# Prompt attention of a hybrid trunk layer: ScalarE scales the mixed values at the head of the next step, VectorE inverts the sums one step sooner

## The reference, cut to what matters

```python
def fox_block(qb, cq, q_pos, k, v, ck, k_pos):
    s = jnp.einsum('bqhd,bshd->bhqs', qb.astype(jnp.float32), k) * DH_F ** -0.5
    s = s + jnp.swapaxes(cq, 1, 2)[..., :, None] - jnp.swapaxes(ck, 1, 2)[..., None, :]
    s = jnp.where(k_pos[None, :] <= q_pos[:, None], s, -jnp.inf)
    p = jax.nn.softmax(s, axis=-1)
    return jnp.einsum('bhqs,bshd->bqhd', p, v).astype(qb.dtype)
```

## Time and profile before

| what | value |
|---|---|
| median of 3 runs | 4860.73 us (4858.03 to 4862.85) |
| the profiled execution | 4847.97 us, of it 4846.3 us from the first to the last instruction |
| granted TensorE clock, mean of the program | 0.929 |
| first attention stage, steps | about 420 to 535 us |
| second attention stage, steps | about 1837 to 2548 us |

### The profile page before, as it was taken

One profiled execution on the slowest core, in us unless ns is written; L12 is line 12 of the kernel. 1 busy time (PEld: TensorE's weight loads), 2 busy tenths in 40 slices (PEclk: granted clock), 3 DMA queues, 4 the chain that ended last, 5 costly groups with the idle time before them and its releaser, 6 DMA issues. The chain is left out here.

```text
span 4846.3 us, 48883 instructions
## 1 busy us (share of the span) xinstructions
PE 4326.4 (89%) x16974; PEld 2666.9 (55%) x16974; DVE 3032.4 (63%) x6385; ACT 969.1 (20%) x1863; POOL 1260.3 (26%) x969
## 2 busy tenths in 40 slices
PE   8996686989999987888887988869999999999988
PEld 5554453665555545666663766654545455444534
DVE  1002351458777767989881487766889777877743
ACT  1112221111101104555541122220000000000023
POOL 0000031014444442333320000004444444444410
PEclk9998788999999997878878999989999999999999
DMA  4443496769999988978858777749999999999941
GB/s 166 144 146 103 143 320 280 279 245 422 379 386 391 374 337 279 343 286 308 331 218 322 291 256 258 239 149 417 419 404 410 419 419 419 415 415 412 412 184 58
DMA packets 363495, 1477.73 MB, mean 305 GB/s; under 512 B 38338, under 2 KB 178418, under 8 KB 242706
## 3 DMA queue, kind: packets, MB, share of 16 engines
q0 software_dynamic: 119872, 824.76, 42.4%
q1 hardware_dynamic: 193874, 625.13, 34.8%
q10 hardware_dynamic: 49536, 25.17, 1.7%
HBM read 1369.00 MB, written 115.38 MB: 306 GB/s over the span
## 5 line engine op out<-in xcount | busy, mean ns | idle before, releaser
L2552 POOL DMA_INDIRECT ex_uv<-in_uv,idx x768 | 1169.7, 1523 | 1706.2 <-DVE ex_acc L2609 1512.5
L2593 DVE CUSTOM_DVE_ANT_0 ex_uv<-ex_uv,ex_xp 128x1024 f32<-128x1024 f32 x768 | 912.8, 1222 | 290.6 <-DMA ex_uv<-in_uv,idx 243.4
L2609 DVE SCALAR_TENSOR_TENSOR ex_acc<-ex_uv,ex_wt,ex_acc 128x1024 f32<-128x1024 f32 x768 | 943.5, 1282 | 10.8 <-DVE C L893 3.2
L392 PE MATMUL proj_psum_acc<-proj_w,aT_later 128*128 128x385 f32 x2304 | 748.8, 487 | 7.7 <-DMA proj_w<-in_w_in 7.7
L2807 PE MATMUL exp_psum_dn<-exp_dn_big,exp_dn_gg 128*128 128x512 f32 x1536 | 685.1, 596 | 28.7 <-DVE exp_dn_gg L2763 28.6
L2798 PE MATMUL exp_psum_dn<-exp_dn_xT,exp_dn_big 128*128 128x384 f32 x2048 | 683.2, 487 | 6.9 <-DMA exp_dn_big<-in_ud 6.9
L392 PEld LDWEIGHTS proj_psum_acc<-proj_w,aT_later 128*128 128x128 f32 x2304 | 437.0, 190 | 319.1 <-DMA proj_w<-in_w_in 7.9
L2798 PEld LDWEIGHTS exp_psum_dn<-exp_dn_xT,exp_dn_big 128*128 128x128 f32 x2048 | 390.0, 190 | 306.4 <-issue 69.5
L2807 PEld LDWEIGHTS exp_psum_dn<-exp_dn_big,exp_dn_gg 128*128 128x128 f32 x1536 | 291.0, 191 | 379.1 <-issue 351.8
L301 PE MATMUL proj_psum_acc<-proj_w,aT 128*128 128x385 f32 x1152 | 377.4, 488 | 4.5 <-DMA proj_w<-in_w_in 2.6
L301 PEld LDWEIGHTS proj_psum_acc<-proj_w,aT 128*128 128x128 f32 x1152 | 218.5, 190 | 159.4 <-issue 5.1
(11 more groups left out here) (460 smaller groups left out, 4241.7 us busy)
## 6 DMA issues: line engine op xcount, KB each, us to landing
proj_w<-in_w_in SPq DMA_DIRECT2D x48, 1540.0 KB, 10.4
rt_w<-in_w_q SPq DMA_DIRECT2D x36, 2048.0 KB, 8.4
exp_dn_big<-in_ud SPq DMA_DIRECT2D x128, 512.0 KB
exp_dn_big<-in_vd SPq DMA_DIRECT2D x128, 512.0 KB
scratch_z<-proj_zs SPq DMA_DIRECT2D x216, 192.5 KB, 2.0
rt_w<-in_w_br_m SPq DMA_DIRECT2D x18, 2048.0 KB, 9.0
rt_w<-in_w_br_f SPq DMA_DIRECT2D x18, 2048.0 KB, 8.9
rt_w<-in_w_out SPq DMA_DIRECT2D x18, 2048.0 KB, 8.0
```

What stands on the lines that cost most here:

```text
L392: mm = pe.matmul(acc[j % SLOTS][:, 0:CW], aT[:, k, t * P:(t + 1) * P], w[:, u % U, k, :], start=(k == 0), stop=(k == KD - 1))
L2552: pool.indirect_dma_start(self.uv[:, slot, :], None, self.uv_tab, bass.IndirectOffsetOnAxis(ap=self.idx[:, at:at + 1], axis=0)).then_inc(s ...
L2593: dve.tensor_tensor_reduce(self.uv[:, slot, 0:D], self.uv[:, slot, 0:D], self.xp[:], 1.0, 0.0, ALU.mult, ALU.add, self.dot[:, g % 2, j:j + ...
L2609: dve.scalar_tensor_tensor(out=self.acc[:, j % 2, :], in0=self.uv[:, slot, D:2 * D], scalar=self.wt[:, g % 2, j:j + 1], in1=self.acc[:, j ...
```

## The change

The scaling leaves VectorE: `act_y` does it on ScalarE with a Copy whose scale is the inverted sum, at the head of turn s+2, ahead of the heads, the mLSTM slot and the copies. The reciprocal stays on VectorE and moves from turn s+2 to turn s+1, behind the maximum of s+1 (`dve_invert`). It now waits for `y_ready` of two steps before, whose buffer of the inverse it writes over. ScalarE's loop has one turn more and VectorE's one less. TensorE, GpSimd and SyncE are as they were.

```diff
-    def dve_y(self, dve, s):
+    def dve_invert(self, dve, s):
+        dve.wait_ge(self.expd, s + 1)
+        if s >= 2:
+            dve.wait_ge(self.y_ready, s - 1)
+        dve.reciprocal(self.inv[:, s % 2:s % 2 + 1], self.total[:, s % 2:s % 2 + 1]).then_inc(self.inverted, 1)
+
+    def act_y(self, act, s):
         hd, b = divmod(s, self.NB)
         i, e = divmod(hd, 2)
-        dve.wait_ge(self.expd, s + 1)
-        dve.reciprocal(self.inv[:, s % 2:s % 2 + 1], self.total[:, s % 2:s % 2 + 1]).then_inc(self.inverted, 1)
-        dve.wait_ge(self.inverted, s + 1)
-        dve.wait_ge(self.mixed, s + 1)
+        act.wait_ge(self.inverted, s + 1)
+        act.wait_ge(self.mixed, s + 1)
         if i >= 2:
-            dve.wait_ge(self.y_out[i % 2], i // 2 * 16)
-        dve.tensor_scalar(self.y[:, i % 2, b, e * DF:(e + 1) * DF], self.y_ps[:, 0:DF], self.inv[:, s % 2:s % 2 + 1],
-                          None, ALU.mult).then_inc(self.y_ready, 1)
+            act.wait_ge(self.y_out[i % 2], i // 2 * 16)
+        act.activation(self.y[:, i % 2, b, e * DF:(e + 1) * DF], self.y_ps[:, 0:DF], ACT.Copy,
+                       scale=self.inv[:, s % 2:s % 2 + 1]).then_inc(self.y_ready, 1)
...
         def _(act):
...
-            for s in range(STEPS + 1):
+            for s in range(STEPS + 2):
+                if s >= 2:
+                    fx.act_y(act, s - 2)
                 if s < STEPS:
                     for hd, g in fx.heads_at(s):
                         fx.act_head(act, hd, g)
                     ml.act_slot(act, *slot(s, 0))
-                if s >= 1:
+                if 1 <= s <= STEPS:
...
         def _(dve):
...
-            for s in range(STEPS + 2):
+            for s in range(STEPS + 1):
                 if s < STEPS:
                     fx.dve_max(dve, s)
-                if s >= 2:
-                    fx.dve_y(dve, s - 2)
+                if s >= 1:
+                    fx.dve_invert(dve, s - 1)
```

## The result

The changed kernel takes 4826.11 us (median of 3 runs, 4822.48 to 4826.2), against 4860.73 before. The ratio is 0.9924, with a 95% interval of 0.9909 to 0.9939.

A forecast was written before the change was run, and what follows sets the result against it. In the second attention stage no single engine bounds, waits between engines decide. 15.3 - 2 + 2 - 2 + 1 = 14.3 us gain: 4833.7 against the profiled execution, 4846.4 us against the median; range 4829 to 4863.

The forecast's parts named there:

- VectorE's side: Second attention stage: without the scaling, VectorE saves 0.30 us in 51 of 95 intervals, 15.3 us, less 2 for new waits.
- TensorE's side: Second attention stage: the 46.7 us wait for `y` all but vanishes, but little reaches the next scores; +2 us.
- act_exp` no longer waits for the reciprocal behind its maximum: Exponentials on ScalarE: dropping their wait for the reciprocal gains under 0.1 us in a dozen steps; +1 us.
- ScalarE's side: Second attention stage: 96 new Copies of 0.31 us, mostly covered by ScalarE's waits for transposes; -2 us.
- The first stage: First attention stage: VectorE half idle, only 2.0 us of waits for `y`; 0 us, between -2 and +2.
- The base: Whole kernel: forecast from one profiled execution, 4847.97 us, with the median shown 12.8 us above it.
- The low end of the range: Whole kernel: 4829 us, given as the middle of the second rival and as what VectorE's upper bound gives.
- the second rival: TensorE, second attention stage: waits for `y` end, granted clock rises above 0.80; gain about 30 us, 4831; chance 0.12.
- VectorE's upper bound: Second attention stage: VectorE's saving of 0.30 us counts in all 96 steps, 28.8 us.
- the signs listed: Profile signs, mainly second stage: VectorE about 28 us less busy, hardly any `y` wait, stage 14 us shorter, clock within 0.03.

## Why the prediction was wrong

**VectorE's side: right, as far as it can be priced alone.** 0.30 us a step was forecast. In the 38 intervals from maximum to maximum that VectorE carries in both timelines, 12.8 us are gone, 0.33 each. The rule of the Trainium skill ("VectorE: DVE Perf Modes", "The DRAIN you can't avoid"), by which a step would save 0.20 us, doesn't hold for these tiny instructions. (The section also says that a next operation which is not held starts earlier; the start 0.07 us behind the reciprocal agrees with that.) Putting the slot back costs 19 us where 15.3 was the term. But the slot's price too depends on the other chains: with the table load held, the kernel that scales on ScalarE is only 6 us ahead of the one that scales on VectorE ahead of the maximum (4842.9 and 4848.4), and with the load free it is 12 (4823.6 and 4835.7). The two differences themselves lie within each other's noise.

**TensorE's side: the step that failed.** "What it wins is the part that reached the next scores", put at +2. The reading of the earlier trace rows was that an earlier mix "would not have brought the next scores forward at all", because they hang on the exponentials. That was true of the timeline as it stood, where mix and exponentials end 0.2 us apart, but the change moves both: by 0.61 and 0.35 us on the mean, and the next scores by 0.44. The other half of the mistake is the term "`act_exp` no longer waits for the reciprocal behind its maximum, worth under 0.1 us in a dozen steps: +1". I priced the reciprocal's 0.15 us, and overlooked that a table load of 1.28 us stands between that wait and the exponentials, and so could never run beside the maximum. The two terms together were 3 us. The reciprocal moved alone brings 20, and `y` ahead of the maximum as well brings 24, all of it still on VectorE (some 5 of either may be VectorE's, by the estimate above); the wait put back into the changed kernel takes 19. What stays open is why the freed wait brings nothing (3 us) while `y` still stands behind the reciprocal, and 20 as soon as it is 0.2 us sooner.

**ScalarE's side: right in kind, perhaps too low.** Forecast -2 for the first Copy; a second one costs 9, at the edge of the noise. The two are not the same thing, since the second comes on top, but it hints that the cover was thin.

**The first stage** was put at 0, and no run contradicts it beyond its error.

**The base** was off as well. Granted TensorE clock and length of the stage vary with the same program: 0.80 and 695.1 us in the earlier trace rows, 0.77 and 0.78 with 709.8 and 706.6 in the other two. Going back from the profiled execution to the median was right, but the counts of waits were those of a short execution, and from their mean the stage lost 30.1 us, not 23.0. The low end of the range doesn't follow from its own reasons either: the second rival stands at 4831, and VectorE's upper bound gives 4860.7 - 28.8 = 4831.9, not 4829. The measured 4826.1 lies below all three.

**Clock.** The second rival (y-waits end, the clock rises, 4831) comes nearest to the outcome; it had 0.12. Of the 30.1 us, TensorE's busy time accounts for up to 18.8: means of 603.2 before and 584.4 after, for the same matmuls. The other 11.3 are time in which TensorE stands idle. The granted clock moved too, but the execution of the earlier trace rows hides it: from 1841 to 2513 us, a stretch inside the stage in all five, it was 0.82, 0.79 and 0.79 before and 0.82 and 0.82 after. So against the two typical executions more of the stage ran at the upper of its two levels, 2.4 instead of 1.2 GHz. Whether the clock drives part of the gain or only follows it, no run separates: no kernel here changes the clock and nothing else. That part stays open.

By the signs listed: VectorE less busy by 26 us (28 forecast), the next instruction 0.07 behind the reciprocal (0.08), waits for scores and Gelu up by 7.9 us (10), hardly any wait for `y`, 128 new Copies of 0.30 us. These came as said, and none of them tells 14 us from 35. The one that does, a second stage 14 us shorter, didn't: it was 23.0. The clock was to move by no more than 0.03. Over the earlier trace rows's stretch it is 0.80 before and after, though 23 us of the next stage's start lie in that stretch now; against the other two executions it is at that limit. The sign that would have told why, the start of the exponentials behind the maximum, was not listed.

## What to carry to other kernels

Where two chains meet at one instruction within a few tenths of a microsecond, price an edit by what it does to both: either alone may bring nothing or half, and an edit that moves one producer (here the reciprocal) may free both. Look at what stands between a wait and the instruction that it is written for: a table load there makes the wait dearer by its own length, and moving the awaited instruction from behind to ahead of a long one hides it. And profile the kernel before more than once when its clock is mixed, since one execution may be 10 us better than the rest (here 4847.97 against 4857.39 and 4859.78).

## What the hardware showed unexpectedly

- A table load starts behind some of the waits of the instruction it is for, and ahead of others: with the reciprocal late it started 0.09 us behind it, and with that semaphore long set it started 0.27 us ahead of the maximum for which its exponentials waited (2241.93 against 2242.20). One number in a wait decides whether a load may run beside the maximum: 29 of 43 start behind its end with one value, 43 of 43 with the other.
- The same program at the same 2882 matmuls has TensorE busy for 590 to 609 us in this stage, from one execution to the next.
- A Copy of 64 columns out of PSUM with its scale in a tile takes 304 ns on ScalarE, against 284 for the same scaling on VectorE.
